# The normalised x of the neighbourhood attention, stored with the grid tokens in front and the meta tokens behind

## The chip, the core and the metric

The kernel runs on one core of a Trainium2 chip. The metric is device time in microseconds; three runs of the kernel before gave 2325.88, 2327.03 and 2327.32 us, with a median of 2327.03.

## What is computed

Two blocks follow each other. The first is causal attention with a pooling branch and a convolutional feed-forward. The second puts 16 meta tokens in front of the 256 tokens of x and runs an even layer (a state space branch and a convolution branch) and an odd layer (neighbourhood attention). The change lies in the odd layer:

```python
def odd_layer(h, norm_g, w_in, rpb, w_out):
    b, L, _ = h.shape                     # L = 16 + 256
    u = rmsnorm(h, norm_g)
    proj = jnp.einsum("bld,de->ble", u, w_in)
    q, k, v, z = split_cols(proj, (NA_WIDTH,) * 4)
    shp = (b, L, NA_HEADS, NA_HEAD_DIM)
    o = neighbourhood_attention(q.reshape(shp), k.reshape(shp), v.reshape(shp), rpb)
    o = o.reshape(b, L, NA_WIDTH) * jax.nn.silu(z)
    return h + jnp.einsum("ble,ed->bld", o, w_out)
```

In the attention every grid token sees its neighbourhood and the 16 meta tokens. The result is `h[:, N_META:]` after a last norm, so that the outputs of the meta tokens are wanted by nobody: q and z are needed on the 256 grid tokens alone, k and v on all 272.

## The kernel before

Tokens lie along the free axis, channels on the partitions. Each of the 16 tiles of a tensor holds 128 channels of all tokens. A projection is computed in float32 accuracy from two halves of each operand: x is split into `xh` (rounded) and `xl` (the rest), a weight chunk into `whi` and `wlo`, and three matmuls stand for one product: `whi` by `xh`, `whi` by `xl`, `wlo` by `xh` (lines 1192 to 1194). A weight chunk is 128 x 1024, so it has 8 tiles of channels and gives 24 matmuls. It comes by a DMA queue into one of 4 `raw` buffers, ScalarE rounds it to `whi` (line 687), and VectorE takes the difference, `wlo` (line 1692), or in the glu, outa and outb stages GpSimd does (line 626). Two chunks make the 16 tiles of one output, which a bank of PSUM collects; VectorE reads it from there.

The stages run in this order: pin, qkv, mix, up, down (first block), then dt, xbc, ssd, glu, outa, outb (even layer), then na (the neighbourhood attention) and naout. In stages with two `joined` matmuls the two halves of x lie side by side and one matmul of 512 columns takes both (lines 1209 and 1210).

`LINE` is 16 elements (64 bytes), `META` 16, `SEQ` 256, `TOK` 272, and `XW` = `TOK` + 3 `LINE` = 320 is the length of one tile in `xhl`. The halves start one `LINE` behind the tensor's head: `xh, xl = xhl[:, LINE:KT * XW], xhl[:, KT * XW + LINE:2 * KT * XW]`. Except in pin and qkv every product reads and writes its columns "by lines": four passes, each of which takes four elements of every line (`by_lines`, the pattern `[4, 4], [LINE, columns / LINE], [1, 4]`). A matmul of 272 columns has 17 lines, one of 256 has 16.

In outb, 8 rounds of 4 chunks produce 16 tiles of the residual. For each tile VectorE adds the bank to x, writes the high half of gain times x to `xh` and the rest to `xl` (function `both`, lines 1716 and 1717) and counts `xs_ready`; ScalarE squares x, and VectorE adds the square to `acc` (line 1728), from which the norm's sum is taken by one matmul (line 1228). The norm's factor is multiplied in later, when a bank is read.

The stage na has 16 pairs of heads. Each pair has 8 chunks, two for each of v, z, q and k. v and k take 272 columns from offset 0 of a tile, z and q 256 columns from offset `META`. Between the chunks stand the small matmuls of the pair before: scores (line 1575), transposes (lines 1585 and 1602), values (line 1595). VectorE puts v and k into the layout of the attention with `keyed`, one operation for the meta columns, which are written several times, and one for the grid columns (lines 2522 and 2523). The first chunk of na waits for the first 8 tiles of the new x, the second for all 16.

The order on each engine is written out by hand, and semaphores count chunks, tiles and steps; `Chain` counts the steps of VectorE that wait for the one ahead, two in each round of outb.

Of the kernel before, what the change touches and what calls it, by code (L numbers as in the profile page):

```python
# [21 lines left out]
META = 16  # L22
SEQ = 256
TOK = META + SEQ
# [6 lines left out]
XW = TOK + 3 * LINE  # L31
# [12 lines left out]
F32 = mybir.dt.float32  # L44
# [5 lines left out]
ADD, SUB, MUL, MAX = ALU.add, ALU.subtract, ALU.mult, ALU.max  # L50
# [65 lines left out]
def program(nc, io):  # L116
    ctx = ExitStack()
    with ctx:
# [16 lines left out]
        x = at("x", KT * TOK)  # L135
        xhl = at("xhl", 2 * KT * XW, F32R)
        gaps = nc.alloc_sbuf_tensor_at("gaps", [P, KT * XW], F32, offset=arena[0] - 2 * KT * XW * 4)
        xh, xl = xhl[:, LINE:KT * XW], xhl[:, KT * XW + LINE:2 * KT * XW]
# [125 lines left out]
        def sem(name):  # L264
            if name not in sems:
                sems[name] = ctx.enter_context(nc.semaphore(name))
            return sems[name]
# [17 lines left out]
        def pbank(phase, k):  # L285
            return bank[(first(phase, 2) + k) % 2]
# [39 lines left out]
        def tok(t, k, i, per, off, n, wide=TOK):  # L326

            if isinstance(i, int):
                o = (per * i + k) * wide + off
                return t[:, o:o + n]  # L330
            return t[:, bass.ds(i * (per * wide) + (k * wide + off), n)]
# [11 lines left out]
        def vcol(name, k=0, i=0, per=0, rows=P):  # L343

            o = VECS[name][0] + k
            if isinstance(i, int):
                return vec[0:rows, o + per * i:o + per * i + 1]
            return vec[0:rows, bass.ds(i * per + o, 1)]
# [821 lines left out]
        def _(pe):  # L1170
# [43 lines left out]
            def ktiles(j, per=2, total=16, size=8):  # L1214
                return range(j % per * size, min(total, (j % per + 1) * size))

            def stream_x(phase, i, j, off=0, n=TOK):
                product(phase, i, j, j // 2, xh, xl, ktiles(j), XW, off, n, j % 2 == 0, j % 2 == 1)
# [191 lines left out]
            for j in range(4):  # L1410
# [7 lines left out]
                out = by_lines(pbank("dt", 0)[:, 0:TOK])  # L1418
# [186 lines left out]
            def na(i, attn, more=True):  # L1605
                for j in range(8):
                    k = j // 2

                    off, n = ((0, TOK), (META, SEQ), (META, SEQ), (0, TOK))[k]
                    if not attn and j < 2:  # L1610
                        pe.wait_ge(sem("xs_ready"), 48 + 8 * (j + 1))
                    if not attn and j == 2:
                        pe.wait_ge(sem("acc_done"), 2 + 80)
                        norm(5)
                    stream_x("na", i, j, off, n)
                    if attn and j == 0:
                        if more:
                            nvalues(i, 1)
                        nscores(i)
                        nvturn()  # L1620
                    if attn and j == 4:
                        nturn(i)
# [56 lines left out]
        def _(dve):  # L1679
            V = nc.vector  # L1680
            ch = Chain(dve, "vector_steps")
# [21 lines left out]
            def freed(phase, i, k, ins):  # L1703

                ins.then_inc(sem("bank_free"), 1)
                dve.wait_ge(sem("bank_free"), tile(phase, i, k) + 3)
# [237 lines left out]
            def residual(phase, ph, off, n, gain=None):  # L1944

                ch.link(V.memset(acc[:, :], 0.0))
                ch.end()

                def finish(i, j, k, from_, ready):
                    landed(i, j, k, from_, ready)  # L1950
                    add_square(k, i * 2 + (16 * ph + k))

                def landed(i, j, k, from_, ready, apart=False):

                    wait_chunk_done(dve, phase, ready, j)
                    xt = tok(x, k, i, 2, off, n)
                    if phase in JOINED and not apart:
                        ch.link(V.tensor_tensor(xt, from_[:, 0:SEQ], xt, ADD))
                        freed(phase, i, k, V.tensor_tensor(xt, from_[:, SEQ:2 * SEQ], xt, ADD))  # L1959
                    else:  # L1960
                        freed(phase, i, k, V.tensor_tensor(xt, from_[:, 0:n], xt, ADD))
                    if phase == "mix":
                        both(xt, *pair_at(t2, k, i, 2),
                             vcol(gain, k, i, 2)).then_inc(sem("xs_ready"), 1)
                    elif gain:
                        both(tok(x, k, i, 2, 0, TOK), tok(xh, k, i, 2, 0, TOK, XW),
                             tok(xl, k, i, 2, 0, TOK, XW), vcol(gain, k, i, 2)
                             ).then_inc(sem("xs_ready"), 1)

                def body(i, last=False, begun=False):  # L1970
                    half = PHASES[phase][1] // 2
                    for j in range(PHASES[phase][1]):
                        if last and phase == "down" and j >= PHASES[phase][1] - LEAD:
                            split_beside(phase, i, j)
                        elif phase != "outb" and not (last and j >= PHASES[phase][1] - LEAD) and not (begun and j == 0):
                            split(phase, i, j)
                        if last and phase == "naout" and j == 3:
                            landed(i, j, 1, pbank(phase, 1), i, apart=True)
                        elif j % half == half - 1:
                            finish(i, j, j // half, pbank(phase, j // half), i)  # L1980

                if phase == "naout":
                    landed(0, 3, 0, pbank(phase, 0), 0)
                    split(phase, 1, 0)
                    add_square(0, 16 * ph)
                    landed(0, 0, 1, pbank(phase, 1), 1)
                    split(phase, 1, 1)
                    add_square(1, 16 * ph + 1)
                    landed(1, 1, 0, bank[2], 1)
                    split(phase, 1, 2)  # L1990
                    add_square(0, 16 * ph + 2)
                    split(phase, 1, 3)
                    finish(1, 3, 1, bank[3], 1)
                    ch.end()
                    with dve.Fori(2, 7) as i:
                        ch.begin(i, 2, 2)
                        body(i)
                    ch.end(5)
                    body(7, last=True)
                    ch.end()  # L2000
                elif phase == "mix":
                    for n_ in range(4):
                        finish(n_ // 2, n_, n_ % 2, (bank[0], bank[1], bank[2], bank[7])[n_], 1)
                        if n_ < 3:
                            split(phase, 1, n_ + 1)
                    ch.end()
                    with dve.Fori(2, 8) as i:
                        ch.begin(i, 4, 2)
                        body(i)
                    ch.end(6)  # L2010
                elif phase == "down":
                    body(0, begun=True)
                    ch.end()
                    with dve.Fori(1, 7) as i:
                        ch.begin(i, 4, 1)
                        body(i)
                    ch.end(6)
                    body(7, last=True)
                    ch.end()
                else:  # L2020
                    with dve.Fori(0, 8) as i:
                        ch.begin(i, 2)
                        body(i)
                    ch.end(8)

# [45 lines left out]
            with dve.Fori(1, 43) as i:  # L2071
# [22 lines left out]
                                           in1=dtc[H, :], op0=ADD, op1=ADD))  # L2094
# [415 lines left out]
            def view(ap, dims):  # L2510
                return bass.AP(tensor=ap.tensor, offset=ap.offset, ap=[ap.ap[0]] + dims)

            def keyed(i, j, k, to, r_):

                wait_chunk_done(dve, "na", i, j)
                from_ = pbank("na", k)
                if to is nvt:
                    meta, rows, dims = [[216, 2], [NS, 4], [1, 4]], [[172, 2], [NS, 4], [1, NC]], [[24, 2], [64, 4], [1, NC]]
                else:
                    meta, rows, dims = [[68, 2], [72, 4], [1, 4]], [[72, 4], [1, 64]], [[64, 4], [1, 64]]  # L2520
                twice = [[0, 2], [4, 4], [1, 4]]
                V.tensor_tensor(view(to[:, 0:META], meta), view(from_[:, 0:META], twice), view(r_[:, 0:META], twice), MUL)
                freed("na", i, k, V.tensor_tensor(view(to[:, 4:TOK], rows), view(from_[:, META:TOK], dims),  # L2523
                                                  view(r_[:, META:TOK], dims), MUL))

            def na(i, attn, more=True):
# [173 lines left out]
```

## Time and profile before

| | |
|---|---|
| median of 3 runs | 2327.03 us |
| span of the profiled execution | 2326.8 us |
| TensorE busy | 2307.9 us, 99% |
| VectorE busy | 1797.4 us, 77% |
| ScalarE busy | 1197.3 us, 51% |
| GpSimd busy | 586.7 us, 25% |
| stage outb | 1719 to 1813 us |
| stage na | 1813 to 2223 us |

The profile is of one execution. Matmuls overlap in it: a row's duration reaches from a matmul's start to its modelled end, and the next one starts long before that. How fast TensorE goes through its matmuls is therefore read from start to start.

### The profile page before, as it was taken

To read this page: it belongs to the slowest core of one execution; us is meant where nothing else is said; L and a number is where in the kernel's file an instruction comes from. 1 tells how busy PE (TensorE), PEld (TensorE's weight loads), DVE (VectorE), ACT (ScalarE), POOL (GpSimd) and SP (SyncE) were. 2 spreads that over 40 slices of the span, in tenths; PEclk is the share of its full clock that TensorE was granted. 3 is DMA by queue.
4 is the path that set the end of the run, shared out by engine and by line. 5 is a ranking of instruction groups with operands and counts; after the bars stand their busy time and mean duration, and the time that the engine had idled before them with its cause. 6 is when DMAs were issued, how large, how long until landed. Compare 5 with 4: busy or idle time off the path is not lost.

```text
span 2326.8 us, 50938 instructions
## 1 busy us (share of the span) xinstructions
PE 2307.9 (99%) x17386; PEld 2191.8 (94%) x17386; DVE 1797.4 (77%) x3192; ACT 1197.3 (51%) x1737; POOL 586.7 (25%) x421
## 2 busy tenths in 40 slices
PE   9999999999999999999999999999999999999997
PEld 9999888989888988899999999999999999999997
DVE  7777888888888766679988889999872566666666
ACT  6444455555555444457766744434544444444444
POOL 0230000000000000013524278888878211111100
PEclk9999999999999999999999999999999999999999
DMA  8544666666666666656655555556555554555444
GB/s 311 189 166 146 201 200 209 205 204 207 201 210 198 212 196 198 191 188 199 185 187 175 181 178 183 180 181 201 176 177 180 186 175 160 169 172 178 161 164 152
DMA packets 153054, 438.20 MB, mean 188 GB/s; under 512 B 32404, under 2 KB 47165, under 8 KB 152845
## 3 DMA queue, kind: packets, MB, share of 16 engines
q1 hardware_dynamic: 149564, 424.70, 55.9%
q0 software_dynamic: 3264, 12.41, 1.9%
q8 instruction: 51, 0.84, 0.2%
q14 instruction: 31, 0.25, 0.0%
q10 hardware_dynamic: 144, 0.02, 0.0%
HBM read 434.88 MB, written 11.09 MB: 192 GB/s over the span
## 4 chain that ended last, share of the span: by engine, by line
PE 92%; DVE 4%; ACT 2%; issue 1%; DMA 1%; SPq 0%; DVEq 0%; ACTq 0%
PE bank L1209 24%; PE bank L1192 17%; PE bank L1194 17%; PE bank L1193 17%; PE bank L1210 12%; DVE wlo L1692 1%; PE bank L1475 1%; ACT whi L687 1%; PE bank L1595 1%; PE bank L1585 1%; DVE c L2141 1%; PE bank L1575 1%; PE bank L1446 0%; DMA raw<-w_up 0%; PE bank L1602 0%
## 5 line engine op out<-in xcount | busy, mean ns | idle before, releaser
L687 ACT CAST whi<-raw 128x1024 fp32r<-128x1024 f32 x784 | 816.0, 1048 | 533.4 <-PE bank L1194 385.1
L1692 DVE TENSOR_TENSOR wlo<-raw,whi 128x1024 fp32r<-128x1024 f32 x620 | 756.8, 1227 | 209.5 <-ACT whi L687 195.5
L1192 PE MATMUL bank<-xhl,whi 128*128 128x272 f32 (+1 forms) x3008 | 854.2, 284 | 1.9 <-DVE nvt L2523 0.8
L1194 PE MATMUL bank<-xhl,wlo 128*128 128x272 f32 (+1 forms) x3008 | 844.4, 281 | 0.0
L1193 PE MATMUL bank<-xhl,whi 128*128 128x272 f32 (+1 forms) x3008 | 844.3, 281 | 0.0
L1192 PEld LDWEIGHTS bank<-xhl,whi 128*128 128x128 f32 x3008 | 565.0, 188 | 4.3 <-DVE nvt L2523 1.0
L1193 PEld LDWEIGHTS bank<-xhl,whi 128*128 128x128 f32 x3008 | 564.9, 188 | 0.6 <-issue 0.2
L1194 PEld LDWEIGHTS bank<-xhl,wlo 128*128 128x128 f32 x3008 | 564.7, 188 | 0.0
L1209 PE MATMUL bank<-xhl,whi 128*128 128x512 f32 x1408 | 470.0, 382 | 0.5 <-DVE ug L2041 0.3
L626 POOL TENSOR_TENSOR wlo<-raw,whi 128x1024 fp32r<-128x1024 f32 x160 | 381.1, 2390 | 93.8 <-ACT whi L687 93.7
L1210 PE MATMUL bank<-xhl,wlo 128*128 128x256 f32 x1408 | 384.4, 273 | 0.0
L1209 PE MATMUL bank<-fhl,whi 128*128 128x512 f32 x960 | 321.1, 383 | 0.4 <-DVE wlo L1692 0.4
L1209 PEld LDWEIGHTS bank<-xhl,whi 128*128 128x128 f32 x1408 | 264.3, 188 | 48.1 <-issue 0.6
L1210 PEld LDWEIGHTS bank<-xhl,wlo 128*128 128x128 f32 x1408 | 264.5, 188 | 0.0
L1210 PE MATMUL bank<-fhl,wlo 128*128 128x256 f32 x960 | 262.1, 273 | 0.0
L593 POOL MEMSET pad<- 128x2 f32 x4 | 0.3, 97 | 836.5 <-DVE dta L2096 836.5
L1209 PEld LDWEIGHTS bank<-fhl,whi 128*128 128x128 f32 x960 | 180.2, 188 | 32.7 <-DVE wlo L1692 0.7
L2368 DVE SCALAR_TENSOR_TENSOR bank<-u,gaps,bank 128x272 f32<-128x272 f32 x448 | 188.9, 500 | 6.6 <-DVE zt L1711 3.3
L1210 PEld LDWEIGHTS bank<-fhl,wlo 128*128 128x128 f32 x960 | 180.4, 188 | 0.0
L587 POOL TENSOR_SCALAR ef<-bc,acsr 128x272 f32<-128x272 f32 (+2 forms) x90 | 98.6, 1108 | 161.4 <-PE bank L1475 157.8
L662 POOL TENSOR_TENSOR btm<-btr,cmask 128x160 f32<-128x160 f32 x64 | 47.0, 766 | 344.1 <-DVE nsc L2476 343.8
L700 ACT ACTIVATE sq<-x 128x272 f32 (+1 forms) x64 | 27.7, 433 | 153.7 <-DVE x L1959 106.8
(302 smaller groups left out, 2793.4 us busy)
## 6 DMA issues: line engine op xcount, KB each, us to landing
raw<-w_up SPq DMA_DIRECT2D x176, 512.0 KB, 4.2
raw<-w_na SPq DMA_DIRECT2D x128, 512.0 KB, 3.6
raw<-w_ssm SPq DMA_DIRECT2D x96, 512.0 KB, 4.2
raw<-w_glu SPq DMA_DIRECT2D x96, 512.0 KB, 3.6
raw<-w_down SPq DMA_DIRECT2D x80, 512.0 KB, 3.7
raw<-w_qkv SPq DMA_DIRECT2D x48, 512.0 KB, 4.2
raw<-w_mix SPq DMA_DIRECT2D x32, 512.0 KB, 3.7
raw<-w_outa SPq DMA_DIRECT2D x32, 512.0 KB, 3.6
```

Source lines behind the costliest of these rows:

```text
L587: ins = G.tensor_scalar(ef[k][0:rows, h * DW + o:h * DW + o + w_], bc[2 * k][0:rows, t0:t0 + w_], acsr[0:rows, c:c + 1], 0.0, SUB, ALU.min)
L626: nc.gpsimd.tensor_tensor(wlo[s][:, :], raw[s][:, :], whi[s][:, :].bitcast(F32), SUB).then_inc(sem("lo_done"), 1)
L662: ins = G.tensor_tensor(by_row(btm, (2 * h + b_) * NK, (4, 0)[b_], NC), from_, m_, ADD)
L687: A.copy(whi[s][:, :], raw[s][:, :]).then_inc(sem("hi_done"), 1)
L700: A.activation(sq[:, k * TOK:k * TOK + TOK], src, ACT.Square).then_inc(sem("sq_done"), 1)
L1192: T.matmul(to_, wh, xh_, start=head, stop=False)
L1193: T.matmul(to_, wh, xl_, start=False, stop=False)
L1194: ins = T.matmul(to_, wl, xh_, start=False, stop=last)
L1209: T.matmul(by_lines(pb_[:, :]), wh, both_, start=head, stop=False)
L1210: ins = T.matmul(by_lines(pb_[:, 0:SEQ]), wl, high_, start=False, stop=last)
L1692: V.tensor_tensor(wlo[s][:, :], raw[s][:, :], whi[s][:, :].bitcast(F32), SUB).then_inc(sem("lo_done"), 1)
L2368: ins = V.scalar_tensor_tensor(out=out, in0=src, scalar=c, in1=acc_, op0=MUL, op1=ADD)
```

## The change

The halves `xh` and `xl` that outb writes for na get their columns in another order: the 256 grid tokens first, the 16 meta tokens behind them. x itself, `acc`, the squares and the norm's factor keep the order with the meta tokens in front. On VectorE `meta_last` writes each half in two pieces. On TensorE z and q read 256 columns from offset 0 of a tile, where they read from offset 16 before; v and k read all 272 as before, so that their banks hold the meta columns at 256 to 271. `keyed` takes them from there.

```diff
-                    off, n = ((0, TOK), (META, SEQ), (META, SEQ), (0, TOK))[k]
+                    n = (TOK, SEQ, SEQ, TOK)[k]
...
-                    stream_x("na", i, j, off, n)
+                    stream_x("na", i, j, 0, n)
...
+                def meta_last(k, i, gain_):
+
+                    xs, xm = tok(x, k, i, 2, META, SEQ), tok(x, k, i, 2, 0, META)
+                    hs, hm = tok(xh, k, i, 2, 0, SEQ, XW), tok(xh, k, i, 2, SEQ, META, XW)
+                    ls, lm = tok(xl, k, i, 2, 0, SEQ, XW), tok(xl, k, i, 2, SEQ, META, XW)
+                    ch.mark(V.tensor_scalar(hs, xs, gain_, None, MUL))
+                    ch.link(V.tensor_scalar(hm, xm, gain_, None, MUL))
+                    V.scalar_tensor_tensor(out=ls, in0=xs, scalar=gain_, in1=hs.bitcast(F32), op0=MUL, op1=SUB)
+                    return V.scalar_tensor_tensor(out=lm, in0=xm, scalar=gain_, in1=hm.bitcast(F32), op0=MUL,
+                                                  op1=SUB)
...
+                    elif phase == "outb":
+                        meta_last(k, i, vcol(gain, k, i, 2)).then_inc(sem("xs_ready"), 1)
...
-                        ch.begin(i, 2)
+                        ch.begin(i, 4)
...
-                V.tensor_tensor(view(to[:, 0:META], meta), view(from_[:, 0:META], twice), view(r_[:, 0:META], twice), MUL)
-                freed("na", i, k, V.tensor_tensor(view(to[:, 4:TOK], rows), view(from_[:, META:TOK], dims),
+                V.tensor_tensor(view(to[:, 0:META], meta), view(from_[:, SEQ:TOK], twice), view(r_[:, 0:META], twice), MUL)
+                freed("na", i, k, V.tensor_tensor(view(to[:, 4:TOK], rows), view(from_[:, 0:SEQ], dims),
                                                   view(r_[:, META:TOK], dims), MUL))
```

TensorE, ScalarE, GpSimd and the DMA queue issue the same instructions in the same order. The one place where instructions are added is VectorE's loop over the rounds of outb. Its queue there before, for one tile:

```order
L1961 TENSOR_TENSOR x<-bank,x 128x272
L1706 ISA
L1716 ISA
L1716 REGISTER_ALU
L1716 TENSOR_SCALAR xhl<-x,vec 128x272
L315 REGISTER_ALU
L1717 ISA
L1717 SCALAR_TENSOR_TENSOR xhl<-x,vec,xhl 128x272
L1726 REGISTER_ALU
L1728 TENSOR_TENSOR acc<-acc,sq 128x272
```

The same place in the changed kernel, where `xhl` is the tensor with both halves, `vec` holds the gain and line 1972 is what line 1961 was:

```order
L1972 TENSOR_TENSOR x<-bank,x 128x272
L1706 ISA
L1958 ISA x2
L1958 TENSOR_SCALAR xhl<-x,vec 128x256
L1959 ISA
L1959 TENSOR_SCALAR xhl<-x,vec 128x16
L315 REGISTER_ALU
L1960 ISA
L1960 SCALAR_TENSOR_TENSOR xhl<-x,vec,xhl 128x256
L1961 ISA
L1961 SCALAR_TENSOR_TENSOR xhl<-x,vec,xhl 128x16
L1728 TENSOR_TENSOR acc<-acc,sq 128x272
```

Each of the two writes has become one of 256 columns and one of 16 right behind it; what stands ahead of them and behind them is the same.

## Rows read from the trace of the kernel before

**Rows 1.** The page: busy time of each engine; TensorE's granted clock in 40 slices.

```profile
PE 2307.9 (99%) x17386; PEld 2191.8 (94%) x17386; DVE 1797.4 (77%) x3192; ACT 1197.3 (51%) x1737; POOL 586.7 (25%) x421
...
PEclk9999999999999999999999999999999999999999
```

**Rows 2.** The waits, TensorE: waiter, awaited, us in total, times, longest.

```profile
PE bank L1192 <- DVE nvt L2523: 0.8, 1, 0.8
```

**Rows 3.** Timeline, TensorE, z and q chunks (start, us, instruction); their group.

```profile
1870.24 0.28 PE L1192 MATMUL bank<-xhl,whi 128*128 128x256 f32 x1
...
1878.51 1.03 PE L1585 MATMUL bank<-ident,nsc 128*88 128x128 f32 x8
...
L1192 PE MATMUL bank<-xhl,whi 128*128 128x256 f32 x24 | 6.6, 276 | 0.0
```

**Rows 4.** Timeline, TensorE, stage pin; groups in the 263 matmuls up to 65.32.

```profile
35.73 0.28 PE L1193 MATMUL bank<-xhl,whi 128*128 128x256 f32 x1
...
65.32 0.28 PE L1193 MATMUL bank<-xhl,whi 128*128 128x256 f32 x1
...
L1193 PE MATMUL bank<-xhl,whi 128*128 128x256 f32 x88 | 24.3, 276 | 0.0
L1194 PE MATMUL bank<-xhl,wlo 128*128 128x256 f32 x87 | 24.0, 276 | 0.0
```

**Rows 5.** Timeline, TensorE, joined matmuls of naout; their group up to 2308.25.

```profile
2238.94 0.39 PE L1209 MATMUL bank<-ohl,whi 128*128 128x512 f32 x1
...
2307.95 0.38 PE L1209 MATMUL bank<-ohl,whi 128*128 128x512 f32 x1
...
L1209 PE MATMUL bank<-ohl,whi 128*128 128x512 f32 x209 | 69.8, 383 | 0.0
```

**Rows 6.** Timeline, TensorE, stage glu; one of three equal groups up to 1620.0.

```profile
1349.22 0.39 PE L1192 MATMUL bank<-xhl,whi 128*128 128x272 f32 x1
...
1620.09 0.28 PE L1192 MATMUL bank<-xhl,whi 128*128 128x272 f32 x1
...
L1192 PE MATMUL bank<-xhl,whi 128*128 128x272 f32 x752 | 212.6, 283 | 0.0
```

**Rows 7.** Timeline, TensorE, outa's last 480 matmuls, outb, first two chunks of na.

```profile
1659.60 0.48 PE L1192 MATMUL bank<-yah,whi 128*128 128x272 f32 x1
...
1718.97 0.28 PE L1192 MATMUL bank<-ybh,whi 128*128 128x272 f32 x1
...
1813.00 0.28 PE L1192 MATMUL bank<-xhl,whi 128*128 128x272 f32 x1
...
1818.87 0.62 PE L1228 MATMUL bank<-acc,ones 128*128 128x272 f32 x2
```

**Rows 8.** Timeline, TensorE, a chunk of qkv: its second matmul and its last.

```profile
93.02 0.28 PE L1193 MATMUL bank<-xhl,whi 128*128 128x256 f32 x1
...
95.61 0.28 PE L1194 MATMUL bank<-xhl,wlo 128*128 128x256 f32 x1
```

**Rows 9.** Timeline: VectorE at outb's last tile; first matmul of na's second chunk.

```profile
1813.31 0.44 DVE L1961 TENSOR_TENSOR x<-bank,x 128x272 f32 x1 [3.66 <-PE bank L1194]
1813.94 0.47 DVE L1716 TENSOR_SCALAR xhl<-x,vec  x1 [0.19 <-DVE x L1961]
1814.56 0.50 DVE L1717 SCALAR_TENSOR_TENSOR xhl<-x,vec,xhl  x1
1814.98 0.43 DVE L1728 TENSOR_TENSOR acc<-acc,sq 128x272 f32<-128x272 f32 x1
...
1815.94 0.28 PE L1192 MATMUL bank<-xhl,whi 128*128 128x272 f32 x1
```

**Rows 10.** Timeline, VectorE, `keyed` of the first pair.

```profile
1825.19 0.18 DVE L2522 TENSOR_TENSOR nvt<-bank,nv 128x32 f32<-128x32 f32 x1
```

## The prediction

> **What bounds the kernel now.** Read the busy shares first: TensorE is busy 2307.9 of 2326.8 us, and its granted clock is full in every slice [rows 1]. In the list of who waited for whom, the stage that the change touches has one wait of a matmul on VectorE's work, 0.8 us, once in 405 us [rows 2]. So no engine behind TensorE can give anything back there; the time is the number of matmuls by the step from one matmul's start to the next. The duration that a group row shows for a matmul (276 to 285 ns) is no measure of that step, since each matmul starts long before the one ahead of it ends. The step has to be taken from start times in the timeline: two starts of an undisturbed run, divided by the number of matmuls between them. That is the view for everything below.
>
> The profiled execution has a span of 2326.8 us, 0.2 us under the median of the runs, 2327.03; the sum is made on the span, and 0.2 us is added at the end.
>
> **The steps as the trace has them.** In pair 2 of the neighbourhood attention the z and q halves run undisturbed for 72 matmuls of 256 columns, from 1870.24 to 1878.51 us: 8.27 / 72 = 114.9 ns [rows 3]. The 256-column matmuls of the pin stage, which read 256 columns in a row, go from 35.73 to 65.32 us in 261 steps: 29.59 / 261 = 113.4 ns [rows 4]. The joined matmuls of the output projection (512 then 256 columns) go from 2238.94 to 2307.95 us in 207 pairs: 333.4 ns a pair, and the columns alone at 2.4 GHz are 768 / 2.4 = 320.0, so 6.7 ns over the columns for each matmul [rows 5]. The 272-column matmuls of the glu stage go from 1349.22 to 1620.09 us in 2256 steps: 120.1 ns, again 6.7 ns over 272 / 2.4 = 113.3 [rows 6]. 256 columns at 2.4 GHz are 106.7 ns, so the pin stage also shows 6.7 over. Three kinds of stream thus stand at the same lowest step, and the 256-column halves of the neighbourhood attention stand 1.5 ns above it (8.2 over the columns). The glu matmuls read the same halves, with the same order by lines and the same start of each tile, 16 elements behind the tensor's head, as the changed halves will; only their width differs.
>
> Steps can also lie above that floor with nobody waiting. The outb stage, which reads its own halves by lines from the same place in a tile, takes 1718.97 to 1813.00 us for 768 matmuls: 122.4 ns; the first two chunks of the neighbourhood attention go on in that step, 5.87 / 48 = 122.3 ns, with the very operands that later run at about 120; and outa, whose tiles are 272 elements long, so that their starts wander over the positions of a line, takes 59.37 / 480 = 123.7 ns [rows 7]. And a chunk of the qkv stage runs at (95.61 - 93.02) / 22 = 117.7 ns where the pin stage has 113.4, with the same form of operands [rows 4, 8].
>
> **The change, part by part.**
>
> *The matmuls.* None is added, removed or moved. 16 pairs x 4 chunks x 24 = 1536 matmuls of 256 columns read from a start one line (16 elements) earlier. The 1536 of 272 columns keep start and width; their columns come in another order, which costs nothing. No row of the trace shows 256 columns by lines from the new start, so the step is bounded from both sides. Lower end: the floor of 113.4, a gain of (114.86 - 113.37) x 1536 = 2.3 us. Upper end: the highest step that 256 columns show, 117.7, a loss of (117.7 - 114.86) x 1536 = 4.4 us. I take the lower end, because the nearest rows are those of glu: same tensor, same start, same order by lines, and they sit on the floor for over 2200 matmuls [rows 6]. What speaks against it is that the width is 16 lines and not 17.
>
> *VectorE in outb.* Each of the 16 tiles of the new x gets four operations for two: 256 and 16 columns for the high halves, and again for the low ones. Before, they take 0.47 and 0.50 us on 272 columns [rows 9]. The nearest small operation is one on 32 columns, 0.18 us [rows 10]. Two of them add at most 0.36 us a tile, 5.8 us of VectorE in all. On the path of the end it is nothing: in each tile VectorE has waited 3.66 us for the matmuls before it starts [rows 9]. Only the last tile has a reader close by: its low half ends at 1814.56 + 0.50 = 1815.06 us, and the second chunk, the first to read it, starts at 1815.94 [rows 9]: 0.88 us of room for 0.36 us. The sum of squares behind it moves from 1815.41 to 1815.8, while the matmul that reads it stands at 1818.87 [rows 7, 9]. The split behind that in VectorE's queue writes the weights of the fourth chunk, which comes after 1818.87 + 2.8. Without that cover the edit would cost 0.36 us once.
>
> *VectorE in the attention.* The meta columns and the grid columns of v and k are taken from the bank at swapped places, with the same two operations (0.18 us for the meta ones [rows 10]). Their count and shapes stay; a read of PSUM from column 0 or 256 in place of 0 or 16 is priced at nothing. The single 0.8 us wait of [rows 2] hangs on the norm and its weights, and stays.
>
> Sum: 2326.8 - 2.3 + 0 + 0 = 2324.5 us of span, 2324.7 us as a median.
>
> **A rule that speaks against it.** The rows show a step of 256 columns that changes between 113.4 and 117.7 without a wait [rows 4, 8]. The Trainium skill (TensorE: Matmul & The Clock Gate, "Step-by-step: what each phase is for") says that TensorE has two independent SBUF read ports, one for the moving operand and one for the weights, and that loading the next weights takes nothing from the running matmul; and "Wait — 56ns, not 53.3ns?" there gives a fixed start to start of the columns plus about 2.5 ns, an estimate of 109.2 ns for 256. The trace disagrees on the size. But if the fixed cost depends on no address, as the rule has it, the new start changes nothing, which is the first rival.
>
> **The rivals.**
>
> *Nothing moves: 2327.0 us.* The 114.9 ns may belong to a 16-line width read by lines in three matmuls, from whichever line it starts. For it: nothing in the trace shows the same width from another start. Against it: joined matmuls of the same width by lines sit on the floor [rows 5]. VectorE's extra work stays hidden in this case too.
>
> *The 272-column chunks fall into the slower step: 2330.5 us.* They follow the 256-column ones, and outb's step was handed on to two chunks of this stage with other operands [rows 7]. If the new halves hand on a rhythm that ends at 122.4 and not at 120.1, the 1488 matmuls of 272 columns behind the first two chunks lose 2.35 ns each: 3.5 us on 2327.0. Even with the gain of the forecast it would be 2328.2.
>
> *The halves take the slow step of qkv: 2331.4 us.* This one ends on the slower side by itself: 117.7 ns on 1536 matmuls, + 4.4 us. Its place is every z and q chunk; it decides as soon as the step lies above 114.9, and reaches 0.2% at 118.
>
> **How the numbers follow.** Floor 0.38 (2324.7); nothing moves 0.32 (2327.0); the 272-column chunks slower 0.11 (2328.2 to 2330.5); the halves slower 0.10 (2331.4, so half of it past 0.2%); both slowdowns or something unseen 0.06 (over 2332); a gain beyond the floor, for instance because the chunks settle sooner, 0.03 (under 2323.8). About 0.2%, 4.7 us, is what a measurement of this kernel can tell from no change. Faster by more: 0.02, since the floor allows 2.3 us. Slower by more: half of 0.10, and 0.06, so 0.08 with some of the latter inside. The range takes the first three cases, with 0.9 us below the forecast for the spread of the runs (1.4 us) and 0.2 above 2330.5: 2323.8 to 2330.7. As cases of both signs hold much of the chance: the forecast's own range is 2323.8 to 2325.8.
>
> **What would show it.** In the changed profile, the z and q chunks of a pair: (start of the transposes - start of the first matmul) / 72 is 113.4 if I am right, 114.9 if nothing moves, 117 or more in the last rival. The k and v chunks of 272 columns: near 120.1 right, near 122.4 wrong. In outb VectorE still waits over 3 us for each tile, and the second chunk starts within 0.05 us of where the first ends. The forecast fails if the step depends on the number of lines and not on where they start, or if it depends on what ran before.

## The result

The changed kernel takes 2333.12 us (median of 7 runs, 2330.49 to 2336.32) against 2326.73 us for the kernel before (7 runs, 2325.88 to 2327.32): a ratio of 1.0029, with a 95% interval of 1.0019 to 1.0038. It is slower by 6.4 us, and its runs spread over 5.8 us where those of before spread over 1.4. The forecast was 2324.7, and its range ended at 2330.7. Two executions in the sets below, one of the kernel before (7654 us) and one of the kernel with shorter splits (4767 us), are in no range and no interval, and move no median by as much as 0.2 us.

Every execution that has both numbers shows a time 1.7 to 1.9 us over its span. The first profile of before, with a span of 2326.8 us, is therefore one of an execution of about 2328.6 us, and the profile of the changed kernel, span 2329.3, one of 2331.1. The two spans differ by 2.5 us only, and have to be compared by stage.

**The step of the z and q chunks went up.** Timeline of the changed kernel, TensorE: first of the 72 matmuls of 256 columns of pair 2 and the end of that run, which answer to [rows 3]; then the first scores of the attention and those of the last pair.

```profile
1870.01 0.28 PE L1192 MATMUL bank<-xhl,whi 128*128 128x256 f32 x1
...
1878.36 0.27 PE L1585 MATMUL bank<-ident,nsc 128*88 128x128 f32 x1
```

```profile
1839.78 0.42 PE L1575 MATMUL bank<-kt,qt 64*128 64x176 f32 x2
...
2230.05 0.42 PE L1575 MATMUL bank<-kt,qt 64*128 64x176 f32 x2
```

The run takes 8.35 us for 72 steps, 116.0 ns, where it took 114.9. From the first scores to the last there are 15 pairs: 390.27 us. In the kernel before the same two starts are

```profile
1840.23 0.42 PE L1575 MATMUL bank<-kt,qt 64*128 64x176 f32 x2
...
2227.55 0.42 PE L1575 MATMUL bank<-kt,qt 64*128 64x176 f32 x2
```

387.32 us, so a pair has become 0.197 us longer, 3.1 us over 16 pairs: some 0.08 in the three chunks of that run, 0.05 in the fourth behind the transposes and 0.06 in the v chunk that precedes the next z, by the starts of the timeline. So some 2 us of the 3.1 come from the 256-column chunks and 1 us from a chunk of 272 columns, whose start and width did not change.

**TensorE waits once for VectorE.** The waits of the changed kernel have a new first row; the 0.8 us wait of [rows 2] is gone from the list. Behind it, the matmuls around that wait:

```profile
PE bank L1192 <- DVE xhl L1961: 2.3, 1, 2.3
```

```profile
1811.05 0.28 PE L1192 MATMUL bank<-xhl,whi 128*128 128x272 f32 x1
...
1813.81 0.28 PE L1194 MATMUL bank<-xhl,wlo 128*128 128x272 f32 x1
1816.37 0.39 PE L1192 MATMUL bank<-xhl,whi 128*128 128x272 f32 x1 [2.28 <-DVE xhl L1961]
```

It is the second chunk of na, which needs the low half of the last tile. In the kernel before it started without a wait [rows 9].

**VectorE is held in outb.** Its groups in 1719.0 to 1816.8 us, 16 tiles:

```profile
L1961 DVE SCALAR_TENSOR_TENSOR xhl<-x,vec,xhl x16 | 24.9, 1557 | 0.0
L1960 DVE SCALAR_TENSOR_TENSOR xhl<-x,vec,xhl x16 | 13.8, 866 | 2.4 <-DVE xhl L1959 1.2
L1958 DVE TENSOR_SCALAR xhl<-x,vec x16 | 13.0, 814 | 4.6 <-DVE x L1972 4.6
L1728 DVE TENSOR_TENSOR acc<-acc,sq 128x272 f32<-128x272 f32 x16 | 11.3, 704 | 0.0
L1959 DVE TENSOR_SCALAR xhl<-x,vec x16 | 7.8, 490 | 0.0
L1972 DVE TENSOR_TENSOR x<-bank,x 128x272 f32 x16 | 7.0, 440 | 13.1 <-PE bank L1194 13.1
```

A write of 16 columns takes 1557 ns on average, more than three times the time of one with 272 before. VectorE's idle time ahead of a tile's addition is 13.1 us in all; before it was 3.66 us at the last tile alone [rows 9]. The timeline with GpSimd beside VectorE shows why. The third tile, and GpSimd's splits beside it:

```profile
1737.23 0.75 DVE L1958 TENSOR_SCALAR xhl<-x,vec  x1 [0.30 <-DVE x L1972]
1737.89 0.22 DVE L1959 TENSOR_SCALAR xhl<-x,vec  x1
1738.27 0.49 DVE L1960 SCALAR_TENSOR_TENSOR xhl<-x,vec,xhl  x1 [0.15 <-DVE xhl L1959]
1738.67 2.36 DVE L1961 SCALAR_TENSOR_TENSOR xhl<-x,vec,xhl  x1
```

```profile
1738.57 5.04 POOL L626 TENSOR_TENSOR wlo<-raw,whi 128x1024 fp32r<-128x1024 f32 x2 [0.75 <-ACT whi L687]
```

GpSimd starts a pair of splits at 1738.57 us. The 16-column write that VectorE starts 0.10 us later ends at 1741.03, about where the first of the two splits does (half of 5.04 is 2.52 us). In other tiles it is the square's addition or a write of 256 columns that takes 2.1 to 2.7 us. The Trainium skill (SBUF — State Buffer, "Who interferes with whom") says that a VectorE instruction with two SBUF inputs contends with a GpSimd instruction that reads SBUF. Of VectorE's 2-port modes, which it says `tensor_scalar` can enter, it says that they contend with GpSimd too, and that whoever issues first gets the shared pair of ports for its whole instruction while the other fully blocks. This trace agrees, and shows the full wait for both kinds: the low half's write, with two tensors as inputs, takes 2.36 us where it takes 0.23 us with no split beside it, and the high half's, with one, takes 2.36 us too (line 1959 at 1806.86 below, against 0.22 above).

In the kernel before the same race was won by a small margin. Its second tile:

```profile
1732.92 0.43 DVE L1728 TENSOR_TENSOR acc<-acc,sq 128x272 f32<-128x272 f32 x1
...
1733.36 4.72 POOL L626 TENSOR_TENSOR wlo<-raw,whi 128x1024 fp32r<-128x1024 f32 x2 [1.18 <-ACT whi L687]
```

VectorE's last two-input operation starts 0.44 us before GpSimd's split; over the 15 tiles that have a split behind them it is 0.24 to 0.52 us, and 0.21 to 0.35 in the second profile of this kernel, whose outb runs at the changed kernel's pace. The changed row is longer. At tile 16, where nothing holds it, 1.98 us pass from the start of the addition to the end of the low half (1814.34 to 1816.32), against 1.75 before (1813.31 to 1815.06 [rows 9]). In the first two tiles its last operation starts 0.05 us behind GpSimd's split and takes 2.6 us. At the end of the stage the holds pile up, because GpSimd's splits come in rows of four there (9.66 us from 1804.37) and not in pairs:

```profile
1806.86 2.36 DVE L1959 TENSOR_SCALAR xhl<-x,vec  x1
1809.37 2.42 DVE L1960 SCALAR_TENSOR_TENSOR xhl<-x,vec,xhl  x1 [0.15 <-DVE xhl L1959]
1811.71 2.35 DVE L1961 SCALAR_TENSOR_TENSOR xhl<-x,vec,xhl  x1
...
1814.34 0.43 DVE L1972 TENSOR_TENSOR x<-bank,x 128x272 f32 x1
...
1816.09 0.23 DVE L1961 SCALAR_TENSOR_TENSOR xhl<-x,vec,xhl  x1
```

Tile 15 is held three times, tile 16 starts only at 1814.34 us, its low half ends at 1816.32, and the matmul follows at 1816.37.

### The profile page after: what moved, and what is told of

Same layout as the page of the kernel before. It is cut to its first block, busy times and chain, and to the rows that moved or that the text cites. A ratio compares the mean times of both kernels' runs of the same rounds, so it can differ in the third digit from the quotient of the medians.

```text
span 2329.3 us, 51010 instructions
## 1 busy us (share of the span) xinstructions
PE 2308.7 (99%) x17386; PEld 2192.9 (94%) x17386; DVE 1842.4 (79%) x3224; ACT 1197.7 (51%) x1737; POOL 590.7 (25%) x421
## 4 chain that ended last, share of the span: by engine, by line
PE 92%; DVE 4%; ACT 2%; issue 1%; DMA 1%; DVEq 0%; SPq 0%; ACTq 0%
PE bank L1209 23%; PE bank L1192 17%; PE bank L1194 17%; PE bank L1193 17%; PE bank L1210 12%; DVE wlo L1692 1%; PE bank L1475 1%; ACT whi L687 1%; PE bank L1595 1%; PE bank L1585 1%; DVE c L2154 1%; PE bank L1575 1%; PE bank L1446 0%; DMA raw<-w_up 0%; PE bank L1602 0%
```

## The experiments

The experiments stood in three sets, each beside its own runs of the kernel before: e1 to e4 (median of before 2326.85 us), e5 to e8 (2328.22) and e9 to e11 (2328.24). Differences are taken within a set.

### One part at a time: the pieces alone

The kernel before, with the four writes in the old places:

```diff
+                    hs, hm = tok(xh, k, i, 2, META, SEQ, XW), tok(xh, k, i, 2, 0, META, XW)
+                    ls, lm = tok(xl, k, i, 2, META, SEQ, XW), tok(xl, k, i, 2, 0, META, XW)
...
-                        ch.begin(i, 2)
+                        ch.begin(i, 4)
```

> The halves keep the order and the starts of before; only the four writes of outb (256 and 16 columns, high and low) are taken over. Theory 1 (held up by GpSimd: a VectorE operation that reads two tensors, met by a running split of GpSimd, waits 2.35 us for it, and the longer row of four runs into the next split): operations of 2.3 us on lines of the writes and of the square in outb, VectorE 30 to 45 us busier, a wait of TensorE on the last tile at the start of the attention, 2 to 8 us, other in each execution; 2329 to 2335 us. The z and q chunks stay at 114.9 ns. Theory 2 (only the start of the halves matters): 2326.7 us, no wait. Theory 3 (the step of the z and q chunks follows from the rhythm that outb hands on): the step changes from 114.9 here too.

Measured: 2329.64 us, 2.8 over before (ratio 1.0013, 1.0004 to 1.0022), with runs from 2327.97 to 2331.97. The held operations are there (line 1961: 24.9 us in 16 tiles), VectorE is busy 1842.4 us, 45 us more than before, TensorE's wait at the second chunk is 2.3 us, and the z and q step stays at 114.9 ns. Theory 1 holds, but for the wait that was to be another in each execution: it is that of the changed kernel. Theories 2 and 3 fall. New is what follows the wait: the clock. Timeline stretches of this profile (us, TensorE busy, granted clock, DMA share, GB/s):

```profile
1816.00:1817.00 1.00, 1.00 (x7) 0.50 0.89 332
1817.00:1819.00 2.00, 2.00 (x10) 0.50 0.84 309
1819.00:1820.00 1.00, 1.00 (x9) 0.95 0.48 152
```

For 3 to 4 us after the wait the matmuls run at the lower of the two levels, 1.2 GHz.

### One part at a time: the start alone

The changed kernel, with `both` on 272 columns back in outb; the reordering is left out.

```diff
-                    elif phase == "outb":
-                        meta_last(k, i, vcol(gain, k, i, 2)).then_inc(sem("xs_ready"), 1)
...
-                        ch.begin(i, 4)
+                        ch.begin(i, 2)
```

> The halves are read from offset 0 as in the changed kernel, but outb writes them with its two operations on 272 columns, so that the tokens stand in the wrong order (left out: the reordering; the outputs are not the reference's). Theory 1 plus an effect of the start: no operation of 2.3 us in outb, no wait at the attention's start, the z and q chunks at 116.0 ns and the first k and v chunk behind them at about 122.7, 0.2 us a pair more than before: 2326.7 + 3 = 2329.5 us, with a spread under 1.5 us. Theory 2 (the start carries all of the loss): 2333 us. Theory 3 (the step follows from outb's rhythm): 114.9 ns and 2326.7 us.

Measured: 2329.16 us, 2.3 over before (1.0009, 1.0000 to 1.0018), with 2.1 us between the lowest and the highest run, where 1.5 was expected. By the times alone this is at the edge of what can be told from no change; the profile decides. No operation is held for the length of a split, no wait stands at the second chunk, and

```profile
1842.66 0.28 PE L1192 MATMUL bank<-xhl,whi 128*128 128x256 f32 x1
...
1851.02 0.27 PE L1585 MATMUL bank<-ident,nsc 128*88 128x128 f32 x1
```

8.36 / 72 = 116.1 ns. The start alone raises the step, and the pair is as long as in the changed kernel. The first chunk of 272 columns behind z and q was expected at 122.7 ns a step; in pair 2 it takes 121.3, as in the kernel before. The two parts are 2.8 and 2.3 us, together 5.1.

### The changed kernel again

> The changed kernel as it is, for a second profile and more times beside the parts. Theory 1: TensorE's wait at the attention's start is another than the 2.3 us of the first profile, with outb's operations of 2.3 us in other tiles; times between 2330 and 2337 us. Theory 2: the same wait and nothing but the steps differs; a spread as small as that of before, 1.4 us.

Measured: 2332.57 us, 5.7 over before (1.0025, 1.0016 to 1.0035), 2330.47 to 2334.38. The wait is again 2.3 us, and VectorE's holds are the same to a few ns: theory 1 was wrong in expecting them in other tiles. What differs from the first profile is the clock behind the wait:

```profile
1816.00:1817.00 1.00, 1.00 (x7) 0.85 0.74 221
1817.00:1819.00 2.00, 2.00 (x11) 0.50 1.03 383
1819.00:1820.00 1.00, 1.00 (x7) 0.50 0.58 127
```

In the first profile of the changed kernel it is 1.00 in all of these stretches:

```profile
1817.00:1819.00 2.00, 2.00 (x19) 1.00 0.98 348
1819.00:1820.00 1.00, 1.00 (x9) 1.00 1.00 283
```

From the first matmul of na to that of the fifth chunk the first profile takes 14.4 us, this one 15.9, the start alone 12.6, and the kernels without the wait lie between 12.0 and 12.9. So the hold costs 1.8 us in an execution that keeps its clock and 3.3 us in one that does not. With the 3.1 us of the pairs that makes 4.9 to 6.4, where the medians say 5.7 here and 6.4 in the result. Whether the clock makes up the changed kernel's spread stays open. Of the seven runs of the result, the two with a mean granted clock of 0.998 took 2330.5 and 2331.1 us and the five with 0.997 took 2332.9 to 2336.3, but the ten of this set are not sorted by it; three executions with the wait were profiled, and in this set the runs of the kernel before spread over 4.5 us themselves (2324.80 to 2329.33).

### Shorter splits on GpSimd

```diff
+                for c in (0, 512):
+                    ins = G.tensor_tensor(wlo[s][:, c:c + 512], raw[s][:, c:c + 512],
+                                          whi[s][:, c:c + 512].bitcast(F32), SUB)
+                ins.then_inc(sem("lo_done"), 1)
```

> The changed kernel, with each of GpSimd's splits in outb cut into two operations on 512 columns. Theory 1: what VectorE waits for lasts half as long, so its held operations in outb come down from 2.35 to about 1.2 us, VectorE's surplus in outb falls to about half, and the wait at the attention's start falls under 1.5 us or goes: about 2329.5 to 2331 us. If GpSimd's operations have nothing to do with it, the held operations stay at 2.35 us and the time at 2333.

Measured: 2329.89 us, 3.0 over before (1.0013, 1.0004 to 1.0022), and the second chunk starts 0.2 us late at most. One tile's last write:

```profile
1739.30 1.25 DVE L1970 SCALAR_TENSOR_TENSOR xhl<-x,vec,xhl  x1
```

The hold is as long as the operation that holds: 1.25 us for 2.36. The total of holds in outb did not fall to half. The five operations from the high half to the square are busy 65.3 us in 16 tiles, for 70.8 in the changed kernel and 27.9 without GpSimd (next experiment): holds of 37 us for 43. But none is long enough to make the last tile late by more than that 0.2 us. What is left is the start's part.

### No GpSimd in outb, and its control

The splits of outb moved to VectorE, in the changed kernel and in the kernel before:

```diff
-            with pool.Fori(0, 8) as i:
-                for j in range(4):
-                    split("outb", i, j)
...
-                        elif phase != "outb" and not (last and j >= PHASES[phase][1] - LEAD) and not (begun and j == 0):
+                        elif not (last and j >= PHASES[phase][1] - LEAD) and not (begun and j == 0):
...
+            dve.wait_ge(sem("lo_done"), chunk("outb", 0, 0) + (LEAD + RING))
             residual("outb", 4, 0, TOK, "g_odd")
```

> The changed kernel with the weight splits of outb on VectorE and none on GpSimd. Theory 1 (a running GpSimd split holds VectorE's two-input operations): no operation of the outb writes is longer than about 0.5 us (0.25 on 16 columns), TensorE's wait of 2.4 us at the second chunk of na goes, and what is left of the loss is that of the start, 0.2 us a pair: about 2.3 to 3 us over before, 2329.5 us. If the four operations are slow by themselves, the 2.3 us operations and the wait stay.

> The kernel before with the weight splits of outb on VectorE, the control of e9_splits_on_vector. Theory 1: GpSimd held nobody up for long in the kernel before, so the time is that of before within 1 us, 2326 to 2328 us, and e9_splits_on_vector lies 2.3 to 3 us above it.

Measured: 2330.70 us for the changed kernel (2.5 over before, 1.0011, 1.0002 to 1.0020) and 2327.70 for the control (0.9999, 0.9990 to 1.0008). Groups of VectorE in outb, changed kernel without GpSimd:

```profile
L1956 DVE SCALAR_TENSOR_TENSOR xhl<-x,vec,xhl x16 | 7.8, 485 | 2.4 <-DVE xhl L1955 1.2
L1954 DVE TENSOR_SCALAR xhl<-x,vec x16 | 5.7, 353 | 4.6 <-DVE x L1968 4.6
L1957 DVE SCALAR_TENSOR_TENSOR xhl<-x,vec,xhl x16 | 3.7, 230 | 0.0
```

The same four operations take 0.35, 0.23, 0.49 and 0.23 us when GpSimd does not split, though VectorE now carries 39 us of splits more. In the control the high half's write on 272 columns takes 0.36 us, where it takes 0.50 on average in the kernel before: GpSimd held that operation a little there too, at the end of its splits. The wait is gone, and the 3.0 us between the two kernels is the start's part, as the steps say (3.1).

### A row longer by one small operation

The kernel before with the high half in two pieces and the low one in one:

```diff
+                    ch.mark(V.tensor_scalar(hs, xs, gain_, None, MUL))
+                    ch.link(V.tensor_scalar(hm, xm, gain_, None, MUL))
+                    return V.scalar_tensor_tensor(out=lt_, in0=xt, scalar=gain_,
+                                                  in1=tok(xh, k, i, 2, 0, TOK, XW).bitcast(F32), op0=MUL, op1=SUB)
```

> The order and the starts of before; in outb only the high half is written in two pieces, the low half in one operation on 272 columns: three operations where before has two and the pieces kernel four. In the kernel before, the square's addition starts about 0.3 us ahead of GpSimd's next split. Theory 1 with that margin: one small operation, 0.22 us, uses most of it up, so that few or some of the operations are held and the wait at the attention's start is 2.4 us or none; 2326.5 to 2329.5 us. If each added operation costs the same, half of the loss of the four pieces: 2328.2 us.

Measured: 2327.79 us (1.0000, 0.9991 to 1.0009). The group that answers to the last of [rows 9]:

```profile
L1728 DVE TENSOR_TENSOR acc<-acc,sq 128x272 f32<-128x272 f32 x16 | 28.8, 1803 | 0.0
```

Already this row is held in most tiles (10 of 16), but what is held is the addition of the square, 1803 ns for 434, behind the low half and not ahead of it. Nobody needs it before the norm, so it costs nothing. The expectation that only some operations would be held was too low. Half the price of the four pieces, 1.4 us, lies inside this interval, which reaches 2.1 us, so the times do not exclude a price by operation. The profile does: the wait at the second chunk is absent, where the four pieces have 2.3 us. Only what stands ahead of `xs_ready` in the last tiles pays.

### The kernel before once more

> The kernel before as it is, for a second profile. In its first profile outb ran at 122.4 ns a step, in every kernel derived from it that was profiled at 120.07, but for one. If that step belongs to the execution and not to the kernel, this profile may have 120.07 in outb, a span of 2325 us and 114.9 ns in the z and q chunks; if it belongs to the kernel, 122.4 and 2326.8.

Its outb:

```profile
1719.82 0.28 PE L1192 MATMUL bank<-ybh,whi 128*128 128x272 f32 x1
...
1812.23 0.28 PE L1192 MATMUL bank<-xhl,whi 128*128 128x272 f32 x1
```

92.41 us for 768 steps, 120.3 ns, where [rows 7] had 122.4. The same kernel runs outb at either step, so the one of 122.4 does not belong to the kernel; whether it goes by the execution or by the chip that it ran on is not shown. The single time is 2327.87 us and the span 2326.1, not the 2325 expected: the stages ahead of outb took 0.85 us longer here. z and q keep their 114.9 and the pair its length in both.

### Where a read starts

Three kernels that differ from before in the place of the halves alone, at 0, 2 and 3 lines behind the tensor's head (before: 1). z and q then start at 1, 3 and 4 lines.

```diff
-        xh, xl = xhl[:, LINE:KT * XW], xhl[:, KT * XW + LINE:2 * KT * XW]
+        xh, xl = xhl[:, HEAD:KT * XW], xhl[:, KT * XW + HEAD:2 * KT * XW]
```

> The kernel before, with both halves of x starting at the tensor's head and not one line behind it: in na the 256-column matmuls read from the same addresses modulo four lines as in the changed kernel, the 272-column ones one line earlier than in either. VectorE's writes and the order of the tokens are those of before. Theory A (the step goes by the address at which the read starts): z and q chunks at 116.0 ns as in the changed kernel, about 3 us more in na, and another step than 120.0 in xbc, ssd and glu, whose 272 columns start elsewhere now. Theory B (it goes by whether z and q start where v and k start): z and q stay at 114.9.

> As e6_head_0, with the halves two lines behind the head (and the convolution weights in the gaps one line later): 272 columns start where 256 did before, 256 one line further on. Theory A: a third step for z and q, between 113.4 and 118 ns, and a changed one for the 272 columns of glu (120.0 before). Theory B: 114.9 and 120.0.

> As e7_head_2, with the halves three lines behind the head, the last of the four positions. Theory A: a fourth pair of steps; if one of these is 113.4 for z and q, the kernel with it would gain 2 us in na, unless the 272 columns lose more in glu (2280 matmuls: 2.3 us for each ns). Theory B: 114.9 and 120.0.

Measured: 2357.85, 2338.50 and 2339.62 us, against 2328.22 (1.0123, 1.0044 and 1.0045). Rows of the three profiles in that order, first the 2280 matmuls of glu, then the 72 of z and q in pair 1; the counterpart of [rows 6] and [rows 3]:

```profile
1358.43 0.39 PE L1193 MATMUL bank<-xhl,whi 128*128 128x272 f32 x1
...
1647.27 0.62 PE L1229 MATMUL bank<-acc,ones 128*128 128x272 f32 x2
...
1867.79 0.28 PE L1193 MATMUL bank<-xhl,whi 128*128 128x256 f32 x1
...
1876.15 0.27 PE L1586 MATMUL bank<-ident,nsc 128*88 128x128 f32 x1
```

```profile
1352.14 0.39 PE L1193 MATMUL bank<-xhl,whi 128*128 128x272 f32 x1
...
1631.37 0.39 PE L1229 MATMUL bank<-acc,ones 128*128 128x272 f32 x1
...
1850.58 0.28 PE L1193 MATMUL bank<-xhl,whi 128*128 128x256 f32 x1
...
1858.81 0.27 PE L1586 MATMUL bank<-ident,nsc 128*88 128x128 f32 x1
```

```profile
1353.81 0.39 PE L1193 MATMUL bank<-xhl,whi 128*128 128x272 f32 x1
...
1633.85 0.39 PE L1229 MATMUL bank<-acc,ones 128*128 128x272 f32 x1
...
1854.59 0.27 PE L1193 MATMUL bank<-xhl,whi 128*128 128x256 f32 x1
...
1862.96 0.27 PE L1586 MATMUL bank<-ident,nsc 128*88 128x128 f32 x1
```

In the first two the other pairs have the step of pair 1. In the third they do not. Its pair 2:

```profile
1880.80 0.28 PE L1193 MATMUL bank<-xhl,whi 128*128 128x256 f32 x1
...
1888.96 0.38 PE L1586 MATMUL bank<-ident,nsc 128*88 128x128 f32 x2
```

8.16 us for 72 steps, 113.3 to 113.4 ns, and so in each of the 14 pairs behind pair 1.

| start, lines behind the tensor's head | 0 | 1 | 2 | 3 | 4 |
|---|---|---|---|---|---|
| 272 columns (glu), ns a step | 126.7 | 120.1 | 122.5 | 122.8 | |
| 256 columns (z, q), ns a step | | 116.1 | 114.9 | 114.4 | 113.4 (116.3 in pair 1) |

Theory A holds, with a remainder. The step goes by where the read starts, in units of 64 bytes, and the two widths have their best places at different lines: what is best for 272 columns, line 1, is the worst for 256 in all pairs but one, and the best for 256 is line 4. The remainder is that one start, in one execution, has two steps, 116.3 ns in pair 1 and 113.4 behind it; what sets it is not shown. z and q starting at line 1 take 116.0 to 116.1 ns, whether the tokens are in the new order or the halves have moved as a whole.

None of these kernels beats the one before. The best place found for z and q, 1.5 ns below, would give 2.3 us (1536 matmuls), and with it stand v and k at line 3, which costs glu alone 2.7 ns on 2280 matmuls, 6.2 us. No run has z and q at line 4 and v and k at line 1.

## Why the prediction was wrong

**What bounds the kernel** was read rightly: TensorE's steps, and one wait. Taking the step from starts and not from durations held in every run.

**The matmuls' term had the wrong sign.** The step that failed: "I take the lower end, because the nearest rows are those of glu: same tensor, same start, same order by lines". The start does matter, but not by itself; it matters together with the number of lines. 17 lines from line 1 stand at the floor; 16 lines from line 1 take 116.0 and, of the starts tried, reach the floor of 113.4 only from line 4. The objection was in the text ("the width is 16 lines and not 17") and was worth more than the rows it was set against. The term is +3.1 us (0.197 us on 16 pairs), where the sum had -2.3. Some 2 us of it are the 256-column chunks and lie inside the bounds that were given, -2.3 to +4.4. The other 1 us is the v chunk ahead of z, 0.06 us longer in each pair, and stood in the sum at nothing.

**The rule that was weighed**, a fixed cost whatever the address, is contradicted by the runs: 6.6 ns lie between the best and the worst start of the same 272 columns.

**VectorE's four operations were priced at their length and covered by idle time, and both were wrong.** The step that failed: "Two of them add at most 0.36 us a tile ... On the path of the end it is nothing". The room of 3.66 us and 0.88 us was read on VectorE alone (and 3.66 is the last tile's; the first has 2.35). GpSimd's splits in the same stage, which read SBUF as VectorE's low halves do, were not looked at; no row of a GpSimd operation stands among those the prediction rests on. In the trace of before a split could be seen starting 0.24 to 0.52 us behind the start of VectorE's last operation in a tile. Where nothing holds the row, it is only 0.23 us longer, less than the 0.36 allowed; what failed is the overlap with GpSimd. The term is +2.8 us in the median, as the pieces alone show, where the sum had 0, and it needed a rival of its own.

**The rivals.** "Nothing moves" fell with the step. "The 272-column chunks fall into the slower step" was right only in a small part: the last chunk of v and k behind z and q is some 0.06 us longer, and the others stay at 120. Its premise, a rhythm handed on from outb, was drawn from one execution; the second profile of before has outb and the first chunks at 120. The prediction's last sign of failure, a step that depends on what ran before, stays possible: pair 1 of the third shifted kernel has another step than the pairs behind it, from the same start. "The halves take the slow step" had the right side and the right place, but 116.0 and not 117.7.

**The profile and the median.** "0.2 us under the median" put the profiled execution beside the median of other executions. By the difference that all others show, its own time was some 1.8 us over its span, about 2328.6, so it was over all seven runs of the result; outb's 2.1 ns by 768 matmuls is 1.6 us of that. This moved the forecast by little, but it made one execution's outb step look like a property of the kernel.

## What to carry to other kernels

Before lengthening a row of operations on VectorE, lay GpSimd's timeline beside it: a row whose last operation starts a quarter to half a microsecond ahead of GpSimd's next long one has no room, however idle VectorE is, and the price comes at the operation that someone waits for. Cutting the long operation in two, or moving it, takes the price away. And a matmul's step at a new start is not to be taken from another width at that start, but from a profile with that start, read in more than one pair.

## What the runs showed of the hardware

- A VectorE operation of 0.23 us on 16 columns takes 2.36 us when GpSimd starts a two-input operation just ahead of it, and 1.25 us when GpSimd's operation is half as long. The first holds for a `TENSOR_SCALAR` with one tensor as input as well as for an operation with two.
- The step of a matmul depends on the 64-byte line at which its moving operand starts: 120.1 to 126.7 ns for 272 columns, 113.4 to 116.1 for 256, with nobody waiting. From one start, line 4, the same kernel took 116.3 ns in one pair and 113.4 in the 14 others.
- After TensorE's wait of 2.3 us its granted clock fell to 0.50 for some 3 to 4 us in two of three profiled executions, which made the wait dearer by 1.5 us.
- The same kernel runs a stage of 768 matmuls at 120.3 or at 122.4 ns a step in different executions.
